# ScalarE copies the product banks of two-strip pairs to SBUF, VectorE adds them later; three of seven blocks in more units of the second pairs; the last two strips become a pair

## The reference, cut to what matters

```
h2  = rms_norm(x, g_mlp)
x   = x + square(relu(h2 @ w_mlp_in)) @ w_mlp_out      # w_mlp_in 2048 x 8192, w_mlp_out 8192 x 2048
out = rms_norm(x, g_final)
```

## Time and profile before

| | |
|---|---|
| time, median of 3 runs | 1630.27 us (1630.06 to 1630.85) |
| time of the profiled execution | 1630.46 us |
| its span in the profile | 1628.6 us |
| PE busy | 1616.6 us (99%) |
| DVE busy | 1215.4 us (75%) |
| ACT busy | 898.4 us (55%) |
| granted TensorE clock | 0.999 over the span |
| PE's waits for other engines in the view of waits | 3.9 us in all, none of them listed after 800 us |

### The profile page before, as it was taken

How to read it: one execution, slowest core, us unless ns; L and a number is a source line. 1 busy time by engine, 2 the same in 40 slices (tenths; PEclk the granted TensorE clock), 3 DMA queues, 4 the chain that set the end, 5 groups by cost and what they waited for, 6 DMA issues and landing times.

```text
span 1628.6 us, 20399 instructions
## 1 busy us (share of the span) xinstructions
PE 1616.6 (99%) x7974; PEld 1361.0 (84%) x7974; DVE 1215.4 (75%) x1470; ACT 898.4 (55%) x1248; POOL 79.0 (5%) x67
## 2 busy tenths in 40 slices
PE   9999999999999999999999999999999999999998
PEld 7888888888888888888888888888888888888886
DVE  7887778877666677766565567996699768986793
ACT  6666656766565445554444555654565455555562
POOL 3000000000000134000000000000000000000000
PEclk9999999999999999999999999999999999999999
DMA  7666665666556664445565775457635863576461
GB/s 270 193 207 201 187 188 188 206 195 205 174 186 185 190 186 154 143 143 179 182 234 193 259 235 190 157 206 235 190 125 202 273 190 130 207 262 189 144 233 52
DMA packets 134192, 312.19 MB, mean 192 GB/s; under 512 B 9744, under 2 KB 10448, under 8 KB 133968
## 3 DMA queue, kind: packets, MB, share of 16 engines
q1 hardware_dynamic: 129376, 302.21, 56.8%
q10 hardware_dynamic: 4720, 8.68, 2.1%
HBM read 308.68 MB, written 2.16 MB: 191 GB/s over the span
## 4 chain that ended last, share of the span: by engine, by line
PE 87%; DVE 9%; issue 2%; DMA 1%; ACT 1%; POOL 0%; POOLq 0%; ACTq 0%; DVEq 0%
PE G L1599 18%; PE G L1600 17%; PE G L1601 17%; PE S L1608 7%; PE G L1608 7%; PE G L1612 4%; PE S L1612 4%; PE S L1599 3%; PE S L1601 3%; PE S L1600 3%; DVE wlo L951 3%; DVE wlo_late L951 2%; PE S L1620 1%; DMA raw<-in_w_in 1%; DVE raw L954 1%
## 5 line engine op out<-in xcount | busy, mean ns | idle before, releaser
L602 ACT ACTIVATE whi<-raw 128x1024 fp32r<-128x1024 f32 x377 | 398.4, 1060 | 395.7 <-PE G L1601 317.0
L951 DVE TENSOR_TENSOR wlo<-raw,whi 128x1024 fp32r<-128x1024 f32 x377 | 461.0, 1236 | 133.6 <-ACT whi L602 132.8
L1599 PE MATMUL G<-whi,a_both 128*128 128x512 f32 x960 | 376.8, 393 | 2.2 <-DVE wlo L951 2.2
L1601 PE MATMUL G<-whi,a_both 128*128 128x512 f32 x960 | 373.8, 389 | 0.0
L1600 PE MATMUL G<-wlo,a_both 128*128 128x512 f32 x960 | 373.8, 389 | 0.0
L1599 PEld LDWEIGHTS G<-whi,a_both 128*128 128x128 f32 x960 | 180.3, 188 | 39.9 <-issue 2.8
L1601 PEld LDWEIGHTS G<-whi,a_both 128*128 128x128 f32 x960 | 180.2, 188 | 37.8
L1600 PEld LDWEIGHTS G<-wlo,a_both 128*128 128x128 f32 x960 | 180.4, 188 | 35.7
L1599 PE MATMUL G<-whi,b_hi 128*128 128x512 f32 x328 | 128.5, 392 | 0.3
L1600 PE MATMUL G<-wlo,b_hi 128*128 128x512 f32 x328 | 128.0, 390 | 0.0
L1601 PE MATMUL G<-whi,b_lo 128*128 128x512 f32 x328 | 127.7, 389 | 0.0
(11 more groups left out here) (283 smaller groups left out, 2591.7 us busy)
## 6 DMA issues: line engine op xcount, KB each, us to landing
raw<-in_w_in SPq DMA_DIRECT2D x208, 512.0 KB, 4.1
raw<-in_w_mlp_in SPq DMA_DIRECT2D x64, 512.0 KB, 4.3
gates<-in_w_mlp_in SPq DMA_DIRECT2D x64, 512.0 KB, 3.7
raw<-in_w_mlp_out SPq DMA_DIRECT2D x64, 512.0 KB, 4.9
gates<-in_w_mlp_out SPq DMA_DIRECT2D x64, 512.0 KB, 4.9
raw<-in_w_ssm_up SPq DMA_DIRECT2D x32, 512.0 KB, 3.6
raw<-in_w_attn_up SPq DMA_DIRECT2D x32, 512.0 KB, 4.0
raw<-in_w_out SPq DMA_DIRECT2D x32, 512.0 KB, 4.6
```

Of the source, the lines that this page charges most:

```text
L602: act.activation(high(m), piece(n), ACT.Copy).then_inc(hi_made, 1)
L951: dve.tensor_tensor(low(m), piece(n), high(m).bitcast(F32), ALU.subtract).then_inc(lo_made, 1)
L1599: pe.matmul(out_ap, hi[:, k, cols], w_hi, start=start, stop=False)
L1601: return pe.matmul(out_ap, lo[:, k, cols], w_hi, start=False, stop=stop)
```

## The change

- The second pairs of groups 0 to 2 cross three units (0, 1, 2) in place of two, and visit their pieces in another order (`PAIR_ORDER[1]`): two pieces of unit 3, units 0 and 1, a third piece of unit 3, unit 2, the last piece of unit 3. The sums of activations are made for three hidden strips (`SUMMED`) in place of two.
- Strips 2 and 3 of group 3 become a pair as well (sort 2), which crosses units 0 and 1. Its last three pieces run per token half (`last_pieces`).
- The mixed banks are no longer added from PSUM by DVE in groups 0 to 2. ACT copies them out in two copies of 128x1024 (`mix_out`, into `m_acc`), and DVE combines them later, during the next group's `mlp_in` windows (`mixed`). For group 3 the old way stays. The plain sums of q=0 (banks G) go out by two ACT copies of 128x1024 into `tmp_both` (`carry_out`), and are added later (`sums`, p=2).
- PE's waits follow: q=1 begins when `m_out` says that the mixed banks of q=0 are copied, its crossed part when `c_out` says that G is copied, and the next `mlp_in` (g, 0) when both copies of q=1's mixed banks are made (`m_out`).
- The ring of raw pieces in the MLP has 7 slots (`LATE_RAW`) in place of 8: the eighth slot's memory holds `s_lo[0]`.
- The load of `g_last` is issued by SP at the start of the last first pair, behind `x_mixed` 6.

```diff
-        window(4 * g + 21 + q, 1, "mlp_pair", (g, q, 1), [("mix", (g, q))])
+        window(4 * g + 21 + q, 1, "mlp_pair", (g, q, 1), [("mix_out", (g, q))])
...
-            window(4 * g + 19, 0, "mlp_in", (g, 0), [("sums", (g - 1, 1))])
+            window(4 * g + 19, 0, "mlp_in", (g, 0), [("sums", g - 1), ("mixed", (g - 1, 0))])
         for j in range(1, 4):
-            window(4 * g + 19 + j // 2, j % 2, "mlp_in", (g, j), [("hidden", (g, j - 1))])
+            window(4 * g + 19 + j // 2, j % 2, "mlp_in", (g, j), [("hidden", (g, j - 1))] + (
+                [("mixed", (g - 1, 1))] if g and j == 1 else []))
         pair(g, 0, [("hidden", (g, 3))])
         if g < 3:
-            pair(g, 1, [("sums", (g, 0))])
-    window(U_END // 2 - 1, 0, "mlp_out", (3, 2), [("finish", 0), ("finish", 1)])
-    window(U_END // 2 - 1, 1, "mlp_out", (3, 3), [("finish", 2)])
+            pair(g, 1, [("carry_out", g)])
+    window(U_END // 2 - 1, 0, "mlp_pair", (3, 1, 0), [("finish", 0), ("finish", 1)])
+    window(U_END // 2 - 1, 1, "mlp_pair", (3, 1, 1), [("mix_out", (3, 1)), ("gain", 0), ("gain", 1), ("finish", 2)])
...
-CROSSED = (1, 2)
-MIX_AT = max(4 * CROSSED[-1] - 4, 0)
+LATE_RAW = LATE_RING - 1
+CROSSED = {0: (1, 2), 1: (0, 1, 2), 2: (0, 1)}
+SUMMED = (0, 1, 2)
+PAIR_ORDER = {
+    0: tuple((unit, part) for unit in range(4) for part in range(4)),
+    1: ((3, 0), (3, 1), (0, 0), (0, 1), (0, 2), (0, 3), (1, 0), (1, 1), (1, 2), (1, 3), (3, 2), (2, 0), (2, 1), (2, 2),
+        (2, 3), (3, 3)),
+    2: ((3, 0), (3, 1), (0, 0), (0, 1), (0, 2), (0, 3), (1, 0), (1, 1), (1, 2), (1, 3), (2, 0), (2, 3), (3, 3), (2, 1),
+        (2, 2), (3, 2)),
+}
+MIX_OUT = {0: 4, 1: 7, 2: 2}
+LAST_PIECES = 3
...
 def piece_slot(n):
-    return n % RING if n < N_MLP else (n - N_MLP) % LATE_RING
+    return n % RING if n < N_MLP else (n - N_MLP) % LATE_RAW
...
-            if p == 5 and j in CROSSED:
-                u = CROSSED.index(j)
-                act.wait_ge(s_v, 4 * (len(CROSSED) * g + u) + 4)
-                act.activation(s_hi[:, u, :, :, :], s_sum, ACT.Copy).then_inc(s_hi_made, 1)
-
-        def mix(p, idx, pr, pp):
+            if p == 5 and j in SUMMED:
+                act.wait_ge(s_v, 4 * (len(SUMMED) * g + j) + 4)
+                act.activation(s_hi[j][:, :, :, :], s_sum, ACT.Copy).then_inc(s_hi_made, 1)
+
+        def wide(t, h):
+            return t[:, 2 * h:2 * h + 2, :].rearrange("p b n -> p (b n)")
+
+        def carry_out(p, g, pr, pp):
+            if p == 0:
+                act.wait_ge(used, done(pr, pp))
+                act.wait_ge(hid_lo, 4 * g + 4)
+                for h in range(2):
+                    act.activation(tmp_both[:, 2 * h * N:2 * (h + 1) * N], wide(G, h), ACT.Copy).then_inc(c_out, 1)
+
+        def mix_out(p, idx, pr, pp):
             g, q = idx
-            if p == MIX_AT:
-                act.wait_ge(used, pair_done(g, q, CROSSED[-1]))
-                if 2 * g + q:
-                    act.wait_ge(x_mixed, 2 * g + q)
+            sort = sort_of(g, q)
+            if p != MIX_OUT[sort]:
+                return
+            act.wait_ge(used, pair_done(g, q, CROSSED[sort][-1]))
+            if sort == 2:
+                act.wait_ge(x_mixed, 7)
+            elif g:
+                act.wait_ge(x_mixed, 2 * (g - 1) + (q + 1))
+            if g == 3:
                 act.activation(mt[:, 0, 0, :], mix_bank(q, 0), ACT.Copy).then_inc(mix_a, 1)
+                return
+            for h in range(2):
+                act.activation(wide(m_acc[q], h), wide(G if q else S, h), ACT.Copy).then_inc(m_out, 1)
...
-        def mix(p, idx, pr, pp):
+        def sums(p, g, pr, pp):
+            if p < 2:
+                dve.wait_ge(used, done(pr, pp))
+                if g:
+                    dve.wait_ge(x_mixed, 2 * g)
+                for tb in range(TB):
+                    part = x_sb[:, 2 + p, tb, :]
+                    dve.tensor_tensor(part, part, sums_bank(1, p, tb), ALU.add).then_inc(c_taken, 1)
+            if p == 2:
+                dve.wait_ge(c_out, 2 * g + 2)
+                own = x_sb[:, 0:2, :, :].rearrange("p a b n -> p (a b n)")
+                dve.tensor_tensor(own, own, tmp_both, ALU.add).then_inc(c_added, 1)
+
+        def mixed(p, idx, pr, pp):
             g, q = idx
             turn = 2 * g + q
-            if p == MIX_AT:
-                dve.wait_ge(mix_a, turn + 1)
+            m, own = m_acc[q], x_sb[:, 2 * q:2 * q + 2, :, :]
+            if p == 4:
+                dve.wait_ge(m_out, 2 * turn + 2)
+                dve.tensor_tensor(m[:, 1, :], m[:, 0, :], m[:, 1, :], ALU.add).then_inc(mix_v, 1)
+                dve.wait_ge(mix_v, 4 * turn + 1)
+                dve.tensor_tensor(m[:, 2, :], m[:, 1, :], m[:, 2, :], ALU.add).then_inc(mix_v, 1)
+            if p == 6:
+                if q:
+                    dve.wait_ge(c_taken, 4 * g + 4)
+                else:
+                    dve.wait_ge(c_added, g + 1)
+                dve.wait_ge(mix_v, 4 * turn + 2)
+                dve.tensor_tensor(own[:, 0, :, :], own[:, 0, :, :], m[:, 0:4:2, :], ALU.add).then_inc(mix_v, 1)
+                dve.wait_ge(mix_v, 4 * turn + 3)
+                dve.tensor_tensor(m[:, 1:3, :], m[:, 1:3, :], m[:, 3, :].unsqueeze(1).to_broadcast([P, 2, N]), ALU.add
+                                  ).then_inc(mix_v, 1)
+            if p == 7:
+                dve.wait_ge(mix_v, 4 * turn + 4)
+                dve.tensor_tensor(own[:, 1, :, :], own[:, 1, :, :], m[:, 1:3, :], ALU.add).then_inc(x_mixed, 1)
+
...
+        def mix_out(p, idx, pr, pp):
+            g, q = idx
+            if g == 3 and p == MIX_OUT[sort_of(g, q)]:
+                dve.wait_ge(mix_a, q + 1)
...
-            if p == MIX_AT + 1:
-                dve.wait_ge(mix_v, 4 * turn + 4)
-                if g:
-                    dve.wait_ge(c_taken, 4 * (turn - 2) + 4)
+                dve.wait_ge(mix_v, 28 + 4 * q)
                 own = x_sb[:, 2 * q:2 * q + 2, :, :].rearrange("p a b n -> p (a b n)")
                 dve.tensor_tensor(own, own, mt[:, :, :, :].rearrange("p a b n -> p (a b n)"), ALU.add
                                   ).then_inc(x_mixed, 1)
...
-        def add_sums(g, q, n):
-            dve.wait_ge(used, pair_done(g, q, 3))
-            dve.wait_ge(x_mixed, 2 * g + q + 1)
+        def add_sums(n):
+            dve.wait_ge(x_mixed, 7)
             for tb in range(TB):
-                part = x_sb[:, 2 * q + n, tb, :]
-                dve.tensor_tensor(part, part, sums_bank(q, n, tb), ALU.add).then_inc(c_taken, 1)
-
-        def sums(p, idx, pr, pp):
-            if p < 2:
-                add_sums(*idx, p)
+                part = x_sb[:, n, tb, :]
+                dve.tensor_tensor(part, part, sums_bank(0, n, tb), ALU.add).then_inc(c_taken, 1)
 
...
         def finish(p, j, pr, pp):
-            late = 5 if j == 2 else j
-            if p == late and j < 2:
-                add_sums(3, 0, j)
-            if p == late and j == 2:
-                dve.wait_ge(used, done(pr, pp))
+            if p == 0 and j < 2:
+                dve.wait_ge(used, pair_done(3, 0, 3))
+                add_sums(j)
+            if p == PIECES - LAST_PIECES and j == 2:
+                dve.wait_ge(used, BLOCK[N_END - LAST_PIECES])
+                dve.wait_ge(x_mixed, 8)
                 for tb in range(TB):
                     part = x_sb[:, j, tb, :]
-                    dve.tensor_tensor(part, part, late_product(pp, tb), ALU.add).then_inc(c_taken, 1)
-            if p == late + 2:
-                dve.wait_ge(c_taken, 26 + 2 * j)
+                    dve.tensor_tensor(part, part, sums_bank(1, 0, tb), ALU.add).then_inc(c_taken, 1)
+            if p == PIECES - LAST_PIECES + 2 and j == 2:
+                dve.wait_ge(c_taken, 14 + 2 * j)
+                for tb in range(TB):
+                    times_gain(j, tb)
+
+        def gain(p, j, pr, pp):
+            if p == 3 + j:
+                dve.wait_ge(used, pair_done(3, 1, CROSSED[2][-1]))
                 dve.wait_ge(s_g_last, 16)
+                dve.wait_ge(c_taken, 14 + 2 * j)
                 for tb in range(TB):
                     times_gain(j, tb)
...
-        def last_window(r, par, idx):
+        def last_pieces():
 
             for tb in range(TB):
-                for p in range(PIECES):
-                    m = BLOCK[piece_number(r, par, p)]
+                for n in range(N_END - LAST_PIECES, N_END):
+                    _, _, unit, part = pair_place(n)
+                    kh, half = PAIR_PARTS[part]
+                    m = BLOCK[n]
                     pe.wait_ge(lo_made, m + 1)
                     for kk in range(2):
-                        cols = slice(kk * N, (kk + 1) * N)
-                        last = three_passes(late_product(par, tb), 2 * p + kk, tb, b_hi, b_lo, high(m)[:, cols],
-                                            low(m)[:, cols], p + kk == 0, 2 * p + kk == KT - 1)
+                        k, cols = 4 * unit + 2 * kh + kk, slice(kk * N, (kk + 1) * N)
```

(58 more changed lines are left out.)

59 lines of the change are left out of this document (28 added, 31 removed).

## The result

The changed kernel takes 1644.78 us (median of 6 runs, 1643.83 to 1646.54) against 1630.2 us: a ratio of 1.009, 95% interval 1.0077 to 1.0103. It is slower by 14.6 us, where +7.9 us was forecast and the range ended at 1642.0. The direction and the places of the waits were right; one term is missing from the sum.

The account below looks back on a forecast made before the run. PE, busy 1616.6 of 1628.6 us, was taken as the bound, with DVE as full in the pairs. Terms -6.8 - 1.2 + 11.4 + 4.5 = +7.9 us on 1630.27 gave 1638.2 us, range 1630.5 to 1642.0.

Parts of the forecast that it names:

- What PE saves: On PE's list, crossed units go from 14 to 19, so 30 matmuls fewer at 0.227 us: -6.8 us.
- the wait that goes: At second pairs' first crossed unit, PE no longer waits for DVE's adds of plain sums, three places: -1.2 us.
- The wait at the end of groups 0 to 2: PE waits before the next `mlp_in` for ACT's copies, queued behind piece 6's split: 3.8 us at three places, +11.4 us.
- The wait in the last pair: In group 3, PE waits before the crossed unit for DVE's four adds of the plain sums: +4.5 us.
- held up by a load, since the ring is shorter: Upper bound of the wait before the last pair's crossed unit: 5.5 us.
- What lies under cover: DVE's late adding in `mlp_in` windows and its tail work were to cost PE 0 us, up to 1.5 for the range.
- The rival of the late tail: DVE bounds the tail too, tb=0's chain pushing tb=1's: +12.8 us, 1643.1 us; chance 0.08.
- The sum: Whole kernel: -6.8 - 1.2 + 11.4 + 4.5 = +7.9 us on the median of 1630.27 us, so 1638.2 us.
- The table of a transfer's cost: Fixed 2.0 us plus bytes at 436 GB/s, 3.2 us for 512 KB; would put the whole sum near +0.7 us.
- The chances: Whole kernel: slower by more than 0.2% (3.3 us) 0.75, within 0.11, faster 0.14; the forecast itself 0.65.
- the upper end: Range's top, 1642.0 us: three group-end waits at 4.6 us and the last pair's at 5.5 are 1641.6.

Follow-up runs that it names:

- e1: Changed kernel, with ACT's copies of q=1's mixed banks in groups 0 to 2 ahead of the splits of step 15: 1635.65 us.
- e2: Changed kernel, with ACT's copies of q=1's mixed banks in groups 0 to 2 ahead of the splits of step 13: 1630.04 us.
- e5: Kernel before the change, with 7 raw slots in the MLP in place of 8 and nothing else: 1632.66 us, ratio 1.0016.
- e3: Changed kernel, with group 3's plain sums too copied out by ACT and added by DVE from SBUF: 1642.75 us.
- e4: Changed kernel with the edits of both e2 and e3: 1627.28 us, ratio 0.9982 to the kernel before.

## Why the prediction was wrong, by its own steps

- *What PE saves, -6.8, and the wait that goes, -1.2.* Right. PE has 30 matmuls fewer, and no hole at the crossed units of the second pairs of groups 0 to 2.
- *The wait at the end of groups 0 to 2, 3 x 3.8.* Right in mechanism, 9.4 us in place of 11.4. In the third group the burst's first load was issued at 1440.42, 1.9 us into unit 2 (1.6 forecast), and its fifth landed about 10.8 us later (11.5 taken). That it is ACT's order was shown by `e1` and `e2`.
- *The wait in the last pair, 4.5.* Right in mechanism, 5.75 measured. VectorE's four adds end 11.1 us after PE starts the pair, where 10.0 was taken from group 2. Its list comes late into the pair, since ACT's copy of the mixed bank stands behind a split that waited for a load; `e5` shows that 7 raw slots alone make such a lateness of 1.2 us. The bound "held up by a load, since the ring is shorter" was the case, and at 5.5 a little low.
- *What lies under cover.* The tail cost nothing, as said: 7.66 us behind PE in both. But it did so only because the holes gave VectorE time. In `e3` and `e4`, with that hole cut to 1.6 and 1.4 us, it is 2.0 us longer. The rival of the late tail was true of the repaired kernel and not of the changed one.
- *The sum.* **Here it failed.** It took a hole in PE's list to cost its length and no more. Behind each of the four holes PE worked for 3.0 to 3.7 us at the lower clock, which cost 6.8 us together, and that is what lies between the sum (+7.9) and the profile (+13.4), less 0.7 us by which the holes were shorter than forecast (+15.2 against +15.9) and 0.5 us ahead of the MLP. The rows of the kernel before could not have given this price. The matmul behind its small hole starts 0.33 us after the one before, not 0.227, but `e1` has the same 0.1 us behind a hole of 1.92 us at a granted clock of 1.00.

The Trainium skill, page "TensorE: Matmul & The Clock Gate", part 1, says that an idle TensorE falls back to half rate and must be busy for a while before it has its full clock again. The traces agree, with a granted clock of 0.50 to 0.55 behind each hole of 2.2 us or more. The forecast drew on no such rule, and it should have: it spoke against this change.

One more thing in the prediction was read too widely. The table of a transfer's cost that it cites from the Trainium skill, page "DMA: Bandwidth & Descriptors", stands in the section "Anatomy of one DMA — SWDGE (gpsimd) path" and is for transfers that GpSimd issues, while SP issues these loads. The sum did not go by it; a lone load took 3.6 us, not 3.2.

The chances gave 0.75 to slower, and 0.65 to the forecast, whose waits came while its sum did not. What was too narrow is the upper end: it stacked the bounds of the waits and had no bound for what follows a wait.

## What to carry to other kernels

Where an engine is 99% busy, ask of each new wait not only how long it is but whether the engine loses its clock by it: four holes of 3 to 6 us cost 15.2 us by themselves and 6.8 us behind them, and holes of up to 1.9 us cost their length and 0.1 us. A copy that frees a bank should stand in its engine's list ahead of everything that waits for a later load; moving two copies by two steps was worth 14.7 us here, more than the arithmetic that the change saved. And a saving found under the cover of a stall has to be looked at again when the stall is gone, as the tail was.

## What the runs showed of the hardware

- Behind holes of 2.2 to 11 us in PE's list, 1.5 to 2.9 us more were lost at the lower clock (granted clock 0.50 to 0.55); behind ones of 1.9 us and less it was 0.1 us at the full clock. The loss did not grow with the hole.
- A lone load of 512 KB takes 3.6 us from issue to landing, the fifth of a burst 5.0 to 6.4 us.
